# Layer norms of a second transformer block made for two halves of the tokens, with the last tiles and the next two slabs split likewise

## The reference

```
h = layer_norm(ALPHA * h + mixer(h) @ w_out, ln_mix_g, ln_mix_b)
h = layer_norm(ALPHA * h + square(relu(h @ w_up)) @ w_down, ln_ffn_g, ln_ffn_b)

def layer_norm(x, g, b):
    mu = mean(x, axis=-1);  var = mean(square(x - mu), axis=-1)
    return (x - mu) * rsqrt(var + 1e-5) * g + b
```

## Time and profile before

| | |
|---|---|
| runs | 2267.11, 2268.79, 2269.73 us; median 2268.79 |
| profiled execution | span 2267.5 us, 29414 instructions |
| TensorE | 2165.4 us busy, 95% |
| weight loads | 1771.0 us, 78% |
| VectorE | 1271.7 us, 56% |
| ScalarE | 885.9 us, 39% |
| granted TensorE clock, mean | 0.970 |

### The profile page before, as it was taken

One profiled execution on the slowest core, in us unless ns is written; L12 is line 12 of the kernel. 1 busy time (PEld: TensorE's weight loads), 2 busy tenths in 40 slices (PEclk: granted clock), 3 DMA queues, 4 the chain that ended last, 5 costly groups with the idle time before them and its releaser, 6 DMA issues.

```text
span 2267.5 us, 29414 instructions
## 1 busy us (share of the span) xinstructions
PE 2165.4 (95%) x11002; PEld 1771.0 (78%) x11002; DVE 1271.7 (56%) x2003; ACT 885.9 (39%) x1298; POOL 84.4 (4%) x91
## 2 busy tenths in 40 slices
PE   6979899999999999999999899999999998999997
PEld 5747778888877888888877688888777776888886
DVE  6986464434455566665566742344568877423444
ACT  4224233222227555565553431242254534312322
POOL 1000300000130000000000000000000000000000
PEclk9989999999999999999989899999999998999998
DMA  4001322233232212222221132222212121322221
GB/s 166 30 10 56 112 75 92 84 103 107 73 116 84 89 49 87 72 86 70 84 83 56 56 101 103 93 93 93 75 56 74 56 93 56 104 101 93 93 93 56
DMA packets 32980, 185.48 MB, mean 82 GB/s; under 512 B 5760, under 2 KB 6144, under 8 KB 14208
## 3 DMA queue, kind: packets, MB, share of 16 engines
q1 hardware_dynamic: 27792, 176.31, 22.6%
q10 hardware_dynamic: 3312, 6.14, 0.8%
q0 software_dynamic: 1792, 1.90, 0.3%
HBM read 180.06 MB, written 2.10 MB: 80 GB/s over the span
## 4 chain that ended last, share of the span: by engine, by line
PE 81%; DVE 10%; DVEq 4%; ACT 2%; issue 1%; DMA 1%; ACTq 0%
PE ps L566 12%; PE ps L567 12%; PE ps L568 12%; PE ps L1047 5%; PE ps L1049 5%; PE ps L1048 5%; PE ps L1098 2%; PE ps L1100 2%; PE ps L1099 2%; PE ps L687 1%; PE ps L627 1%; PE ps L617 1%; PE ps L984 1%; PE ps L967 1%; PE ps L980 1%
## 5 line engine op out<-in xcount | busy, mean ns | idle before, releaser
L1268 ACT ACTIVATE w_hi<-raw 128x2048 fp32r<-128x2048 f32 (+1 forms) x122 | 226.1, 1853 | 298.6 <-PE ps L568 220.2
L566 PE MATMUL ps<-x_hi,w_lo 128*128 128x512 f32 x816 | 317.6, 389 | 0.5 <-DVE y L2185 0.3
L568 PE MATMUL ps<-x_hi,w_hi 128*128 128x512 f32 x816 | 317.5, 389 | 0.0
L567 PE MATMUL ps<-x_lo,w_hi 128*128 128x512 f32 x816 | 317.4, 389 | 0.0
L1708 DVE TENSOR_TENSOR w_lo<-raw,w_hi 128x2048 fp32r<-128x2048 f32 (+3 forms) x116 | 259.2, 2235 | 93.9 <-ACT w_hi L1268 93.6
L1047 PE MATMUL ps<-x_hi,w_lo 128*128 128x512 f32 x544 | 218.9, 402 | 2.4 <-DVE w_lo L2337 2.4
L1049 PE MATMUL ps<-x_hi,w_hi 128*128 128x512 f32 x544 | 213.2, 392 | 0.0
L1048 PE MATMUL ps<-x_lo,w_hi 128*128 128x512 f32 x544 | 212.3, 390 | 0.0
L566 PEld LDWEIGHTS ps<-x_hi,w_lo 128*128 128x128 f32 x816 | 153.2, 188 | 33.0 <-issue 0.7
L568 PEld LDWEIGHTS ps<-x_hi,w_hi 128*128 128x128 f32 x816 | 153.2, 188 | 31.9
L567 PEld LDWEIGHTS ps<-x_lo,w_hi 128*128 128x128 f32 x816 | 153.2, 188 | 31.6
(11 more groups left out here) (452 smaller groups left out, 4050.3 us busy)
## 6 DMA issues: line engine op xcount, KB each, us to landing
raw<-w_attn_in SPq DMA_DIRECT2D x32, 1024.0 KB, 4.9
raw<-w_gate_up SPq DMA_DIRECT2D x22, 1024.0 KB, 4.9
raw<-w_up_a SPq DMA_DIRECT2D x16, 1024.0 KB, 4.8
raw<-w_down_a SPq DMA_DIRECT2D x16, 1024.0 KB, 4.9
raw<-w_up_h SPq DMA_DIRECT2D x16, 1024.0 KB, 4.9
raw<-w_down_h SPq DMA_DIRECT2D x16, 1024.0 KB, 4.9
raw<-w_hgrn_in SPq DMA_DIRECT2D x8, 1024.0 KB, 4.8
raw<-w_down SPq DMA_DIRECT2D x8, 768.0 KB, 4.3
```

What stands on the lines that cost most here:

```text
L566: pe.matmul(o, w_lo[:, slot, a:a + P], hi[:, k, :], start=k == 0, stop=False)
L567: pe.matmul(o, w_hi[:, slot, a:a + P], lo[:, k, :], start=False, stop=False)
L568: last = pe.matmul(o, w_hi[:, slot, a:a + P], hi[:, k, :], start=False, stop=k == st.kc - 1)
L1268: act.activation(w_hi[:, slot, 0:width], raw[:, slot, 0:width], ACT.Copy).then_inc(whi_ready, 1)
```

## The change

All four layer norms of the second block are made in two halves of the tokens, `TOKENS` (0 to 255, 256 to 511).

- Late tiles. `LATE` holds the last two tiles of the stage ahead for mix, the last one for ffn. TensorE makes their first halves (256 columns, `late_bank` half 0: the two usual banks), then their second halves (banks 2 and 3). A late tile's first half waits for t-1 adds in paired stages too.
- VectorE folds only the tiles before them; the late tiles are shifted ahead. The fold's sums stand 4 chunks before the end of the last late tile's first half.
- `late_sums` and `late_spread` are made once for each half: of the first half within the second halves of the late tiles, of the second half within the first two slabs of the next stage (`LATE_SUMS`, `LATE_SPREAD`).
- VectorE runs over the 8 chunks twice. Within the first half stand the adds of the second halves (after chunk 1), half of the second slab's `w_lo` (after 3), mean and variance of the second half (after 4), its reciprocal and the rest of that `w_lo` (after 5). Both halves of the first slab's `w_lo` now stand before the first late add.
- ScalarE too runs twice; after `x_hi` of chunk 1 stand the squares of the second half and the split of the second slab.
- TensorE begins the next stage with `first_halves` in `HALF_ORDER` in place of the pair and the triple: both slabs with all 8 chunks of the first half, then of the second.
- SP stores 16 halves instead of 8 chunks.

```diff
-                 ("up_a", 8), ("hgrn_in", 8), ("hgrn_out", 8), ("up_h", 8)])
+                 ("up_a", 16), ("hgrn_in", 16), ("hgrn_out", 8), ("up_h", 16)])
+    LATE = {"mix": (6, 7), "ffn": (7, )}
+    HALF_ORDER = (((0, 0), (0, 1), (0, 2), (0, 3), (1, 0), (1, 1), (0, 4), (1, 2), (0, 5), (1, 3), (1, 4), (0, 6), (1, 5),
+                   (0, 7), (1, 6), (1, 7)),
+                  ((0, 0), (0, 1), (0, 2), (1, 0), (0, 3), (0, 4), (1, 1), (0, 5), (0, 6), (1, 2), (0, 7), (1, 3), (1, 4),
+                   (1, 5), (1, 6), (1, 7)))
+    LATE_SUMS, LATE_SPREAD = (0, 1), (0, 6)
...
+    def late_bank(st, t, half):
+        return 2 + t % 2 if half else (st.tile0 + t) % 2
...
+            def first_halves(st, event, part, layer):
+                ...
+                for half, tokens in enumerate(TOKENS):
+                    for c, k in HALF_ORDER[half]:
+                        slot, js = (st.slab0 + c) % 2, range(st.cum[c], st.cum[c + 1])
+                        if c == 0:
+                            pe.wait_ge(xhi_ready, XB[event] + DC * half + k + 1)
+                        elif (half, k) == (0, 0):
+                            read_out(before, st)
+                            pe.wait_ge(whi_ready, st.slab0 + 2)
+                        ...  # w_hi * x_hi, 256 columns
+                        if (half, k) == (0, 0):
+                            pe.wait_ge(wlo_ready, st.slab0 + c + 1)
+                        ...  # w_lo * x_hi
+                        if c == 0:
+                            pe.wait_ge(xlo_ready, XB[event] + DC * half + k + 1)
+                        ...  # w_hi * x_lo
+                        if half == 0 and (c, k) == LATE_SUMS:
+                            late_sums(part, layer, 1)
+                        if half == 0 and (c, k) == LATE_SPREAD:
+                            late_spread(part, layer, 1)
...
-                        pe.wait_ge(tile_free[st.reader], st.free0 + t - (3 if paired else 1))
+                        pe.wait_ge(tile_free[st.reader], st.free0 + t - (3 if paired and t < late[0] else 1))
...
+                    if (t, k) == (late[-1], st.kc - 4):
+                        pe.wait_ge(root_ready, SK[mean] + 1)
+                        pe.wait_ge(folded, nth + 1)
+                        token_sum(MEAN, acc, True, False)
+                        token_sum(SUM, acc_sq, True, False)
...
+                    if (t, k) == (late[0], 4):
+                        late_sums(part, layer, 0)
+                    if (t, k) == (late[-1], st.kc * (3 - len(late)) // 2 - 4 * (2 - len(late)) - 1):
+                        late_spread(part, layer, 0)
...
+                for t in late:
+                    await_slab(t)
+                    tile(t, late_bank(st, t, 0), TOKENS[0], fold, late_done)
+                for t in late:
+                    tile(t, late_bank(st, t, 1), TOKENS[1], first_half_sums, tile_done)
...
+            def normed(layer, part, n, after, second):
+                for half, tokens in enumerate(TOKENS):
+                    for c in range(DC):
+                        ...  # h and x_hi of this half
+                        if (half, c) == (0, 1):
+                            late_squares(layer, part, 1)
+                            if second:
+                                second()
+                        if (half, c) == (0, 4):
+                            late_root(layer, part, 1)
...
+                    for c in range(DC):
+                        tt(y[:, c, tokens], y[:, c, tokens], scale, ALU.mult).then_inc(y_ready, 1)
+                        ...
+                        if (half, c) == (0, 1):
+                            late_tiles(st, layer, part, 1)
+                        if after and (half, c) == (0, 3):
+                            second_lo("hgrn_in" if after == "hgrn_in" else after + "0", 0)
+                        if (half, c) == (0, 4):
+                            late_variance(layer, part, 1)
+                        if (half, c) == (0, 5):
+                            late_invert(layer, part, 1)
+                            if after and after != "hgrn_in":
+                                second_lo(after + "0", 1)
```

More of the change, by code:

```diff
@@ L263, in build @@
     SPREAD_MEAN = 4
-    SPREAD = {"pre_mix": SUM, "ssm": 3, "post_mix": 5, "pre_ffn": 4, "post_ffn": 5,
-              "var_mix_a": 5, "var_ffn_a": 5, "var_mix_h": 5, "var_ffn_h": 5}
+    SPREAD = {"pre_mix": SUM, "ssm": 3, "post_mix": 5, "pre_ffn": 4, "post_ffn": 5}
+    SPREAD.update({f"{what}_{part}_{layer}": 5 for layer in "ah" for part in ("mix", "ffn") for what in ("var", "late")})
     NTH_SPREAD = {name: k for k, name in enumerate(SPREAD)}
@@ L300, in build @@
     MEANS = {name: k for k, (name, _) in enumerate(ACCS[2:])}
+    LATE_AT = counts([(f"{part}_{layer}", 2 * len(LATE[part])) for layer in "ah" for part in ("mix", "ffn")])
     PR = {name: k for k, name in enumerate(
@@ new lines, in block_sum, with late_spread @@
+            def block_sum(bank, src, half, stop):
+                for b in range(TB)[BLOCKS[half]]:
+                    last = pe.matmul(ps[:, bank, b:b + 1], src[:, b * P:(b + 1) * P], one, start=False, stop=stop,
+                                     skip_group_check=True)
+                return last
+            def late_spread(part, layer, half):
+                nth = 2 * MEANS[f"mean_{part}_{layer}"] + half
+                var = (f"var_{part}_{layer}", f"late_{part}_{layer}")[half]
+                mean_bank, scale_bank = spread_banks(part, layer, half)
+                pe.wait_ge(mean4_ready, nth + 1)
+                if half and mean_bank == SPREAD_MEAN:
+                    pe.wait_ge(y_ready, YB[f"res_{part}_{layer}"] + DC)
+                spread_blocks(mean_bank, mean4, half).then_inc(mean_spread, 1)
+                pe.wait_ge(rstd_ready, SK_ROOT[var] + 1)
+                spread_blocks(scale_bank, rstd4, half).then_inc(rstd_spread, 1)
@@ L649, in out_chunk, with dense @@
                         last.then_inc(tile_done, 1)
-            def dense(name, operand=None, xs=None, hid=None, beside=None, begun=0):
+            def dense(name, operand=None, xs=None, hid=None, beside=None, begun=0, behind=None):
                 st = STAGES[name]
+                if behind:
+                    first_halves(st, operand, *behind)
+                    with pe.Fori(1, st.trips) as i:
+                        for c in range(len(st.body)):
+                            slab(st, c, i)
+                    return
                 if name in PAIRED:
@@ L2453, in layer_norm @@
                 settle()
-                dve.wait_ge(sq_used, SB[var] + DC)
-                stt(var4, ps[:, SUM, 0:TB], 1.0 / D, var4, ALU.mult, ALU.subtract).then_inc(var4_ready, 1)
-                if part == "mix":
-                    next_lo(STAGES[{"a": "attn_out", "h": "hgrn_out"}[layer]], 1)
-                dve.wait_ge(root_ready, SK[var] + 1)
-                dve.reciprocal(rstd4, root4).then_inc(rstd_ready, 1)
-                dve.wait_ge(mean_spread, nth + 1)
-                for c in range(2):
-                    tt(y[:, c, :], y[:, c, :], mean, ALU.subtract)
@@ L2490, in norm_and_ffn @@
                 normed_out(f"{down}1", layer, "ffn")
-                layer_norm(layer, "ffn", n, after)
+                layer_norm(STAGES[f"{down}1"], layer, "ffn", n, after)
             a0, b0 = GAIN_AT["lb0"], GAIN_AT["lb1"]
```

283 lines of the change are left out of this document (168 added, 115 removed).

## The result

The changed kernel takes 2286.9 us (median; 2283.4 to 2288.0), the kernel before 2268.8 on the same chip: ratio 1.0076, 95% interval 1.0061 to 1.0090. It is slower, as forecast, but by 18 us and not by 5.9, and outside the range (2262 to 2285).

A forecast was written before the change was run, and what follows sets the result against it. TensorE was taken as the bound (95% busy, 81% of the chain). Two mix places +6.2 us, ffn +0.5 and the end -0.8 made +5.9 on 2268.8: 2274.7 us, own range 2271 to 2279, with rivals 2262 to 2285.

The forecast's parts named there:

- a trial: Check of the clock: 0.213 us per short product over 7 us in late tiles or pair moves the end by nothing.
- (b): Mix place, fold: VectorE has folded at 1878.1, TensorE waits 1.6 us for it, before 2.4.
- (d): Mix, pair's first half: VectorE and ScalarE set the pace; w_lo ready 1.6 us later than before, TensorE waiting 2.7 for it.
- Rival (3): Clock stays at 0.5 from late tiles into the pair: 4.5 us more per mix place, 1.2 at ffn, 2285; chance 0.12.
- (a): Mix place, ahead of tile 6's first half: TensorE newly waits 3.6 us for tile 4's add on VectorE.
- (e): Mix, pair: TensorE waits 8.3 us inside the first half; 12 groups of 6 short products follow w_lo, ending at 1922.5.
- (c): Mix, fold to next stage: late halves and sums follow; TensorE's first product comes at 1889.3, 5.2 us ahead of before.
- (f): Mix, end of the pair: TensorE waits 1.1 us for the next slab's split, whose next product comes 3.1 us later.
- The short product: TensorE's price for a product of 256 columns: taken as 0.114 us, with a ceiling of 0.121.
- ffn: First layer's ffn place, one late tile: first product 5.5 us sooner, 9 us of waits, +0.5 us in all.
- The end: Last norm and stores: last result at 2264.5 against 2265.0, last store half as large, -0.8 us in all.

The follow-up runs named there:

- d_warm: Kernel before with only spare 512-column products added in TensorE's waits at the norm places: 2265.2 us, ratio 0.9985.
- w_pair3: Changed kernel with spare products ahead of waits in the next stage's first two slabs, 3 ahead of the second slab's first products at mix: 2279.2 us.
- w_late: Changed kernel with 15 spare 512-column products in the wait ahead of tile 6's first half at both mix places: 2287.5 us.
- s_spread: Changed kernel with the second half's statistics spread one chunk sooner in TensorE's order, behind chunk 5 instead of 6: 2282.8 us.
- ws3: w_pair3 with the sooner second spread of s_spread: 2280.8 us.
- w_pair2: Changed kernel with spare products ahead of waits in the next stage's first two slabs, 18 ahead of the second slab's first products at mix: 2284.0 us.
- d_warm2: d_warm with 12 instead of 10 spare products ahead of the fold and 8 instead of 4 between spreads at the first mix place: 2263.1 us.

## Why the prediction was wrong in size, and where it was right

The step that failed is the last sentence ahead of the sum: "a trial with 0.213 us per short product over 7 us in either place moves the end by nothing, since the waits of (b) and (d) swallow it". The clock stayed at 0.5 for 13 us in the pair (1907.5 to 1920.6), and 5.7 us of them lie behind the wait for w_lo, the last that could swallow anything; so 7 us, put where the waits are, could only give nothing. Rival (3) comes nearest, with 4.5 us at each mix place and 1.2 at ffn, 2285 in all; measured over the forecast are 4.2, 4.5 and 2.7. It was held at 0.12. But it names other products: a clock that stays at 0.5 from the late tiles into the pair. In the second layer's place it didn't stay. What the text held against the rival, dense work behind (a), did bring it back: the short products of 1892.80 to 1895.43 are 0.12 us apart. It fell anew inside the pair, whose waits step (e) itself puts at 8.3 us. That rival (3)'s price fits the mix places is luck. The kernel before gave a warning: its TensorE stands idle for 3.2 of 16.0 us from 1882 to 1898, and the clock is 0.5 all through (the row under d_warm).

Where the miss lies, place by place (mix, ffn, mix): from the pair's first product to the next slab 2.0, 2.0 and 3.0 us over the forecast, of which w_pair3 takes away 1.5, 2.0 and 2.5 by keeping the clock up. Ahead of the pair it is 2.3, 0.6 and 1.6. At ffn the clock is 1.00 up to the pair (1622.58 to 1637.49), so the 0.6 is not the clock; the price of the short products and of the first ones under (c) accounts for it. What the mix places have beyond that goes with their stretches at 0.5, behind (a) and, in the first layer's, behind the fold (0.50 from 1258.6 to 1260.0); w_late filled the wait of (a) and the clock fell further on, so no run shows what that part would cost at full clock.

- (a): right. 3.54 and 3.57 us of wait. The wait itself cost nothing, for the fold bound; the cold products behind it brought the fold's sums 1.1 us later than VectorE allowed in the second layer's place and 0.3 in the first (w_late).
- (b): the fold has no wait in the changed kernel, since (a)'s products ran at 0.213; folded 1889.83, sums 1890.90. That is 1.3 us later behind tile 5 than worked out, 0.4 in the first layer's place.
- (c): the first product of the pair starts 22.3 to 23.0 us behind tile 5, forecast 20.7, before 25.9. It is 2.9 to 3.6 us ahead of before, not 5.2. One more cause beside the clock: the first product behind sums or a spread takes 0.20 us, not 0.12.
- (d): right. x_hi of chunk 2 behind the 1.9 us split, w_lo 12.5 us after the pair's first product (12.75 forecast). TensorE waits 1.9 us for it, not 2.7.
- (e): the waits are there, but of 8.3 us TensorE stood idle for 4.4 (12.56 us with 8.14 busy, 1902.40 to 1914.96), since cold products filled the rest. Of the "12 groups of 6 short products" at 0.114, some 26 took 0.213 each.
- (f): right, 0.9 us for 1.1.
- The short product costs 0.120 us (36 in 4.32 us, 2256.21 to 2260.53, clock 1.0), not 0.114: the ceiling was the better guess, and by the text's own sum that is worth nearly 3 us. By the Trainium skill ("TensorE: Matmul & The Clock Gate", "Back-to-back issue gap"), whose formula is for a single product, it would be 0.109; the row decides. One number of that part of the prediction is slightly off: 1868.63 to 1874.08 for 24 is 0.227 and not 0.2266, which changes no sum by more than 0.1 us.
- ffn: +3.2 for +0.5. The clock was 0.5 from 1645.6 to 1650.0, behind the last wait of the first half, and here VectorE's second half hangs on TensorE's spread (s_spread), so that each us of delay is paid in full.
- The end: -0.5 for -0.8, right within 0.3.

Open: why the clock falls at one mix place and not at the other with the same instructions (late tiles of w_pair3, 23.0 against 21.5 us; behind w_lo in ws3) was not settled; 1 to 1.5 us a place hang on it. Spare products between the first two chunks of the pair were not tried, as no bank is free there while VectorE adds the late halves.

## What to carry to other kernels

A change that cuts one long wait into several short ones inside a stream of products is to be priced with the clock at 0.5 until well behind the last of them; lay the trial's cold stretch over the part where TensorE is the bound, not over the waits. Read the granted clock of such stretches in the profile before: where it is 0.5 and TensorE sets the end, spare products that fill the waits ahead of it may be worth more than a new order of the work. Count and place them so that they end before the wait does; 2.0 us too many cost 1.9 (w_pair2), and in ws3 the same number of them as in w_pair3 left a wait of 2.0 us behind which the clock fell again.

## What the runs showed of the hardware

- The granted clock stayed at 1.2 GHz through 5.6 us (1914.96 to 1920.60) in which TensorE was busy without a gap, and products that TensorE need not make shorten a place by 3.3 us (d_warm2) when they keep it at 2.4. The Trainium skill ("TensorE: Matmul & The Clock Gate", "HAM oscillation — how this bites in real kernels") prices time at the lower clock at half its length. That would be 2.8 us here for 5.6; measured are 2.5 (8.10 against 5.61), so the trace agrees roughly.
- Behind a product of 256 columns that follows one-column sums or a spread, the next starts 0.20 us later, not 0.12 (1892.60 to 1892.80 against 1892.80 to 1892.92 in the changed kernel).
- The same instructions gave 21.5 or 23.0 us between tile 5 and the pair, by where the clock fell; so the place's own times scatter by 1.5 us between kernels that don't differ there, and edits must be read from the pair on.
